# Lengths of keys and queries in the DeltaNet mixer: from a matrix of ones times the squares, in place of diagonal matrices of inverse lengths

## The reference, cut to what matters

```python
def _l2norm(x):
    xf = x.astype(jnp.float32)
    return (xf * lax.rsqrt(jnp.sum(xf * xf, axis=-1, keepdims=True) + EPS)).astype(x.dtype)

    b_qkv = jax.nn.silu(_dwconv_centred(b_qkv, conv_w))
    qb, kb, vb = jnp.split(b_qkv, 3, axis=-1)
    qb = _l2norm(qb.reshape(bsz, T, H_B, DK))
    kb = _l2norm(kb.reshape(bsz, T, H_B, DK))
```

## Time and profile before

| | |
|---|---|
| median of 3 runs | 1379.74 us (1378.78 to 1380.05) |
| the profiled execution | 1380.04 us |
| its span | 1378.3 us |
| PE busy | 1338.7 us (97%), 10242 instructions |
| DVE, ACT, POOL busy | 400.3, 282.4, 108.3 us |
| HBM | 499.86 MB, mean 363 GB/s |
| chain that ended last | PE 92%, DMA 4%, DVE 2%, ACT 1%, issue 1% |

### The profile page before, as it was taken

How to read it: one execution, slowest core, us unless ns; L and a number is a source line. 1 busy time by engine, 2 the same in 40 slices (tenths; PEclk the granted TensorE clock), 3 DMA queues, 4 the chain that set the end, 5 groups by cost and what they waited for, 6 DMA issues and landing times.

```text
span 1378.3 us, 23298 instructions
## 1 busy us (share of the span) xinstructions
PE 1338.7 (97%) x10242; PEld 705.6 (51%) x10242; DVE 400.3 (29%) x517; ACT 282.4 (20%) x364; POOL 108.3 (8%) x182
## 2 busy tenths in 40 slices
PE   4999999999999999999999999999999999999987
PEld 2997677678888885333333333333333333333332
DVE  2856344666444454101201400401101100100213
ACT  2673534453344333000000000000000000000011
POOL 6200141324000001000000000000000000010010
PEclk9999999999999999999999999999999999999998
DMA  9854967988777779999999999999999999999995
GB/s 382 306 161 152 379 252 277 405 311 301 244 244 245 260 293 416 363 360 427 427 423 430 427 422 412 424 410 430 424 426 429 425 425 427 428 423 427 425 428 239
DMA packets 103750, 499.86 MB, mean 363 GB/s; under 512 B 10514, under 2 KB 14303, under 8 KB 74855
## 3 DMA queue, kind: packets, MB, share of 16 engines
q1 hardware_dynamic: 87664, 471.75, 84.7%
q10 hardware_dynamic: 13590, 18.29, 3.7%
q0 software_dynamic: 2400, 8.42, 1.5%
HBM read 478.74 MB, written 19.69 MB: 362 GB/s over the span
## 4 chain that ended last, share of the span: by engine, by line
PE 92%; DMA 4%; DVE 2%; ACT 1%; issue 1%; ACTq 0%; DVEq 0%; SPq 0%
PE ps L2523 21%; PE ps L2520 17%; PE ps L2550 15%; PE ps L458 5%; PE ps L460 5%; PE ps L459 5%; PE ps L2557 4%; DMA ring_a<-in_moe_down 3%; PE ps L1927 3%; PE ps L1913 2%; PE ps L2059 1%; PE ps L2060 1%; PE ps L2061 1%; PE ps L2203 1%; PE ps L2016 1%; DMA raw<-in_w_mod 1%
## 5 line engine op out<-in xcount | busy, mean ns | idle before, releaser
L399 DVE TENSOR_TENSOR w_lo<-raw,w_hi 128x2048 fp32r<-128x2048 f32 x60 | 144.8, 2416 | 124.2 <-ACT w_hi L395 124.2
L2523 PE MATMUL ps<-ring_a,hTf 128*32 128x512 f32 (+1 forms) x1488 | 146.7, 551 | 0.0
L395 ACT ACTIVATE w_hi<-raw 128x2048 fp32r<-128x2048 f32 x59 | 112.8, 1914 | 108.7 <-PE ps L460 99.8
L2520 PE MATMUL ps<-raw,hTf 128*64 128x512 f32 (+1 forms) x624 | 123.8, 552 | 0.9 <-DMA raw<-in_moe_up 0.9
L1862 DVE TENSOR_TENSOR hm<-gate_bc,ps 32x384 f32<-32x384 f32 (+1 forms) x56 | 34.0, 607 | 267.5 <-PE ps L2520 266.6
L1868 DVE TENSOR_TENSOR hm<-gate_bc,ps 128x384 f32<-128x384 f32 (+1 forms) x16 | 9.4, 588 | 345.5 <-PE ps L2523 345.3
L2523 PEld LDWEIGHTS ps<-ring_a,hTf 128*32 128x32 f32 x1488 | 47.9, 110 | 96.9 <-issue 93.9
L458 PE MATMUL ps<-w_hi,hTh 128*128 128x512 f32 x232 | 91.5, 394 | 0.0
L460 PE MATMUL ps<-w_lo,hTh 128*128 128x512 f32 x232 | 90.4, 389 | 0.0
L459 PE MATMUL ps<-w_hi,hTl 128*128 128x512 f32 x232 | 90.3, 389 | 0.0
L2520 PEld LDWEIGHTS ps<-raw,hTf 128*64 128x64 f32 x624 | 44.1, 137 | 78.0 <-issue 74.9
(11 more groups left out here) (429 smaller groups left out, 1776.1 us busy)
## 6 DMA issues: line engine op xcount, KB each, us to landing
raw<-in_w_mod SPq DMA_DIRECT2D x48, 1024.0 KB, 7.8
raw<-in_moe_down SPq DMA_DIRECT2D x22, 2048.0 KB, 22.6
ring_a<-in_moe_down SPq DMA_DIRECT2D x20, 2048.0 KB, 19.1
ring_a<-in_moe_up SPq DMA_DIRECT2D x14, 2048.0 KB, 18.8
raw<-in_moe_gate SPq DMA_DIRECT2D x13, 2048.0 KB, 18.3
ring_b<-in_moe_down SPq DMA_DIRECT2D x13, 2048.0 KB, 19.5
ring_a<-in_moe_gate SPq DMA_DIRECT2D x11, 2048.0 KB, 24.6
raw<-in_moe_up SPq DMA_DIRECT2D x10, 2048.0 KB, 15.5
```

The lines of the kernel that those rows point to most:

```text
L395: nc.scalar.activation(w_hi[:, w % SPLIT], raw[:, slot % RAW], ACT.Copy).then_inc(s["hi_ready"], 1)
L399: nc.vector.tensor_tensor(w_lo[:, w % SPLIT], raw[:, slot % RAW], w_hi[:, w % SPLIT].bitcast(F32), ALU.subtract).then_inc(s["lo_ready"], 1)
L2520: last = MM(ps[HB * j:HB * j + HB, part % 4, 0:w], xT[:, kt, HB * (g // 2):HB * (g // 2) + HB], wt[:, kt % 2, 2 * (g % 2) + j, :], start=k ...
L2523: last = MM(ps[TOK * j:TOK * j + TOK, part % 4, 0:w], xT[:, KT * g + kt], wt[:, kt % 2, j, :], start=kt == 0, stop=kt == KT - 1)
```

## The change

The sums are spread at once: PE multiplies the matrix of ones, now the stationary side, with 512 columns of squares, which gives the sum over the channels in every partition. ACT takes square roots of 128x1024 from PSUM to `XT`, keys and queries apart, DVE takes reciprocals of 128x1024 in place, and multiplies. The diagonal matrices (DVE and POOL), `spread_lengths`, and the semaphores `len_diag`, `len_inverse`, `len_turned` go. On DVE the multiplications now stand ahead of `unit_lo` 14 and 15.

```diff
-            pool.wait_ge(s["len_inverse"], 1)
-            nc.gpsimd.tensor_tensor(XT[:, 0:8], rep(ident[:, :], 1, 8), rep(sm[:, 17, 0:8], 2, P), ALU.mult)\
-                .then_inc(s["len_diag"], 1)
...
             unit_hi(act, 13)
-            act.wait_ge(s["ss_turned"], 2)
-            nc.scalar.activation(sm[:, 16], ps[:, 6, 0:16], ACT.Sqrt, bias=eps[:, 0:1]).then_inc(s["rq_ready"], 1)
+            for first, bank in ((8, 2), (0, 6)):
+                act.wait_ge(s["ss_turned"], 1 if bank == 2 else 2)
+                nc.scalar.activation(flat2(XT[:, first:first + 8]), flat2(ps[:, bank:bank + 2]), ACT.Sqrt, bias=eps[:, 0:1])\
+                    .then_inc(s["rq_ready"], 1)
             copy_proj(5)
...
+            qv = b_ch[:, 0:4].rearrange("p a (c n) -> p (a c) n", n=P)
+            kv = b_ch[:, 4:8].rearrange("p a (c n) -> p (a c) n", n=P)
             dve.wait_ge(s["rq_ready"], 1)
-            nc.vector.reciprocal(sm[:, 17], sm[:, 16]).then_inc(s["len_inverse"], 1)
-            dve.wait_ge(s["len_inverse"], 1)
-            VT(XT[:, 8:16], rep(ident[:, :], 1, 8), rep(sm[:, 17, 8:16], 2, P), ALU.mult).then_inc(s["len_diag"], 1)
+            step(nc.vector.reciprocal(XT[:, 8:16], XT[:, 8:16]))
+            VT(kv, kv, XT[:, 8:16], ALU.mult).then_inc(s["kn_ready"], 1)
+            dve.wait_ge(s["rq_ready"], 2)
+            step(nc.vector.reciprocal(XT[:, 0:8], XT[:, 0:8]))
+            nc.vector.scalar_tensor_tensor(qv, qv, DK ** -0.5, XT[:, 0:8], ALU.mult, ALU.mult).then_inc(s["qn_ready"], 1)
             unit_lo(dve, WOUT)
             unit_lo(dve, WOUT + 1)
...
-            dve.wait_ge(s["len_turned"], 1)
-            VT(kv, kv, inv[:, 8:16], ALU.mult).then_inc(s["kn_ready"], 1)
-            dve.wait_ge(s["len_turned"], 2)
-            nc.vector.scalar_tensor_tensor(qv, qv, DK ** -0.5, inv[:, 24:32], ALU.mult, ALU.mult).then_inc(s["qn_ready"], 1)
...
-            def square_sums(first):
+            def square_sums(first, bank):
 
                 pe.wait_ge(s["sq_ready"], 1)
+                pe.wait_ge(s["cols_saved"], 4)
                 pe.wait_ge(s["diff_ready"], 2)
-                for i in range(first, first + 8):
-                    last = MM(ps[:, 6, i:i + 1], X[:, i], ones[:, 0:1], start=True, stop=True)
+                for h in range(2):
+                    last = MM(ps[:, bank + h, :], ones[:, :], flat(X[:, first + 4 * h:first + 4 * h + 4]), start=True, stop=True)
                 last.then_inc(s["ss_turned"], 1)
-
-            def spread_lengths():
-
-                pe.wait_ge(s["len_diag"], 2)
-                pe.wait_ge(s["cols_saved"], 4)
-                for i, bank in ((2, 2), (3, 3), (0, 6), (1, 7)):
-                    last = MM(ps[:, bank, :], ones[:, :], flat(XT[:, 4 * i:4 * i + 4]), start=True, stop=True)
-                    if i % 2:
-                        last.then_inc(s["len_turned"], 1)
...
                         if n == 10:
-                            square_sums(8)
-                        if n == 12:
-                            spread_lengths()
+                            square_sums(0, 6)
...
                 if i == 4:
-                    square_sums(0)
+                    square_sums(8, 2)
```

More of the change, by code:

```diff
@@ L157 @@
 hc_lo hi_ready hT_by_scalar hT_by_vector htok_turned k_saved k_turned kd_ready kdf_ready kn_ready ks_turned
-ktok_saved ktok_turned kv_y_stored L_beta L_masked L_turned late_saved late_sel late_turned len_diag
-len_inverse len_turned lo_ready logits_saved logits_turned LT_saved m1_saved m1_turned mask_ready
+ktok_saved ktok_turned kv_y_stored L_beta L_masked L_turned late_saved late_sel late_turned
+lo_ready logits_saved logits_turned LT_saved m1_saved m1_turned mask_ready
 mod_cols_saved mod_cols_turned mod_rows_copied mod_used mx_ready o_b_turned o_turned oa_ready p_exp p_in
@@ L1484, in _ @@
                 unit_lo(dve, i)
+            qv = b_ch[:, 0:4].rearrange("p a (c n) -> p (a c) n", n=P)
+            kv = b_ch[:, 4:8].rearrange("p a (c n) -> p (a c) n", n=P)
             dve.wait_ge(s["rq_ready"], 1)
-            nc.vector.reciprocal(sm[:, 17], sm[:, 16]).then_inc(s["len_inverse"], 1)
-            dve.wait_ge(s["len_inverse"], 1)
-            VT(XT[:, 8:16], rep(ident[:, :], 1, 8), rep(sm[:, 17, 8:16], 2, P), ALU.mult).then_inc(s["len_diag"], 1)
+            step(nc.vector.reciprocal(XT[:, 8:16], XT[:, 8:16]))
[3 more added lines that the diff above has]
+            nc.vector.scalar_tensor_tensor(qv, qv, DK ** -0.5, XT[:, 0:8], ALU.mult, ALU.mult).then_inc(s["qn_ready"], 1)
             unit_lo(dve, WOUT)
             unit_lo(dve, WOUT + 1)
-            qv = b_ch[:, 0:4].rearrange("p a (c n) -> p (a c) n", n=P)
-            kv = b_ch[:, 4:8].rearrange("p a (c n) -> p (a c) n", n=P)
-            inv = ps.rearrange("p a (c n) -> p (a c) n", n=P)
-            dve.wait_ge(s["len_turned"], 1)
-            VT(kv, kv, inv[:, 8:16], ALU.mult).then_inc(s["kn_ready"], 1)
-            dve.wait_ge(s["len_turned"], 2)
-            nc.vector.scalar_tensor_tensor(qv, qv, DK ** -0.5, inv[:, 24:32], ALU.mult, ALU.mult).then_inc(s["qn_ready"], 1)
             dve.wait_ge(s["decay_ready"], 2)
```

## The result

The changed kernel takes 1381.8 us (median of 20 runs, 1379.87 to 1383.44), the kernel before 1379.45 us (20 runs). The ratio is 1.0014, 95% interval 1.0008 to 1.0020: 1.1 to 2.8 us slower, small, but clear of no change. I had forecast 0.3 us less, and no measurable change. The profiled execution took 1381.64 us with a span of 1379.9.

What follows compares the result with a forecast made beforehand. PE alone was taken to bound 98 to 153 us. It saves 3.57 us and gives back 3.2 waiting for DVE, net 0.3: profiled 1380.04 to 1379.7, median 1379.4, stated as 1379.5; range 1378.3 to 1384.0 us.

Steps and rivals of the forecast that it cites:

- PE's own saving: On PE, `spread_lengths` goes and ones products replace the one-column sums: 3.57 us saved, all on the chain.
- ACT and POOL at nothing: ACT's larger square roots fit ahead of its copy at 113.0 and POOL's dropped 2.93 us were hidden: no cost, no gain.
- The reciprocals, D = 6.2 us: On DVE, each of two 128x1024 reciprocals takes 6.2 us, from slopes of narrow rows carried to 1024 columns.
- My own formula, 2 x (D - 6.36): Net time change in us from D, the time of one wide DVE reciprocal, down to a floor of -3.57.
- The place where PE would wait, and on what: PE waits 1.2 us for `qn_ready` ahead of `key_products(0)`, then 2.0 us for DVE's `L_masked` ahead of `key_products(1)`.
- The dearer reciprocal, 8.7 us: Rival: a wide DVE reciprocal makes eight passes a column, 8.7 us each, +4.7 us, time 1384.4; chance 0.16.
- Softmax just in time: DVE's later list still lets `turn_probs(1)` and `turn_probs(2)` start in time, within 0.3 us; costed at nothing to 0.3.
- Moved units hidden: `unit_lo` 14 and 15 move later on DVE, delaying two modulation loads 9 and 6.6 us; hidden with 5 us over.
- PE's clock: Rival: PE's new gaps lower its granted clock behind `L_masked`, losing 1.7 us, time 1381.1; chance 0.10.
- the prediction's signs of being wrong: Reciprocals' mean over 7.7 or under 4.8 us, `turn_probs(1)` starting later than before, or granted clock falling in 133 to 140.

Runs made afterwards that it cites:

- ln_exp: Changed kernel with DVE's reciprocals replaced by ScalarE computing exp(-0.5 ln(sum + eps)); ratio 0.9983 to the kernel before, span 1376.9 us.
- units_later: Changed kernel with `unit_lo` 14 and 15 moved behind `mask_keys(0)` on DVE; ratio 1.0004 to the kernel before, span 1379.6 us.
- fill_first: Changed kernel with two unused products added on PE only in its first gap, ahead of `key_products(0)`; ratio 1.0013 to the kernel before, span 1379.7 us.
- fill_second: Changed kernel with two unused products added on PE only in its second gap, ahead of `key_products(1)`; ratio 1.0021 to the kernel before, span 1381.3 us.
- extra_512: Changed kernel with one more reciprocal of 128x512, of values no longer read, on DVE ahead of `unit_lo` 14; ratio 1.0046 to the kernel before, span 1385.0 us.
- fill_both: Changed kernel with four unused products added on PE, two in each of its two gaps; ratio 1.0006 to the kernel before, span 1380.1 us.
- after_again: The changed kernel traced a second time with nothing altered, to see whether the clock's fall repeats; span 1378.0 us.
- widths: Changed kernel with reciprocals of eight widths (8 to 1024 columns) and some products added after all DVE work; time not compared, 1024 against 512 columns 3198 ns more.

## Why the prediction was wrong, step by step

- **PE's own saving, 3.57 us: right.** `ln_exp` shows it whole, 3.56 us at both `key_products`.
- **ACT and POOL at nothing: right.** The two roots ran from 108.87 to 110.99 and ScalarE still idled 1.80 us before its next copy.
- **The reciprocals, D = 6.2 us: the term that was mis-sized.** They took 6.55 each. My own formula, 2 x (D - 6.36), gives +0.4 for that, and the traces without a clock loss on the path show +0.4 to 0.5 at `hTh`. Both of my slopes, 6.1 and 5.7 ns, lay under 6.25: carried to 1024 columns they gave 6.4 and 6.0 us, the 6.2 between them lies under the 6.36 at which the sign turns, and the measured 6.55 lies over it. The rows could not decide the sign. From 4 columns (176 ns) to 16 the row of 252 ns gives 6.3 ns a column and 6.6 us, that of 246 ns gives 5.8 and 6.1 us: 6 ns between two rows of 16 columns become 0.5 us at 1024, and 1 us in the result. So the forecast of 0.3 us less was inside what the rows left open. The place where PE would wait, and on what, was right: the two gaps were forecast as 1.2 and 2.0 us and came as 1.98 and 1.74, the beta products and mask at 129.9 and 132.2 in place of 129.2 and 131.5.
- **The dearer reciprocal, 8.7 us: refuted.** The Trainium skill, VectorE: DVE Perf Modes, section "Walkthrough: the 8-slice pipeline in each mode", speaks of a repeat count of 8; read as eight passes it would be 8.35 ns a column, and 6.25 were measured. The measurement decides: six times an ordinary product's 1.04, not eight.
- **Softmax just in time: right.** `turn_probs(1)` and `(2)` had no wait on DVE in the changed kernel.
- **Moved units hidden: right** at their place, with little over, as `units_later` shows by moving them 3.5 us further.
- **PE's clock, left out of the sum, with a chance of 0.10 and 1.7 us: the size was right, the chance too small.** I had one row, a gap of 2.51 us, and took gaps of 1.2 and 2.0 as mostly safe. In the traces here, gaps of 1.7 to 2.0 us were followed by a fall in four of seven traces (the changed kernel two of three, `fill_first` one of one, `fill_second` one of two, `units_later` none of one); `extra_512`, with 5.4, fell as well. It costs time on the path only if PE's list is the last to arrive behind it. One of the prediction's signs of being wrong is this fall in 133 to 140; it came in the first trace. The other that came is `turn_probs(1)`, which starts at 143.72 there and at 142.29 and 142.23 in the other two traces, in place of 141.71.

The sum of both, 0.4 and a larger part of 1.7, would lie inside the measured 1.1 to 2.8 us. But only one of three traces paid the clock's 1.7 us on the path; as a mean that makes 0.4 + 0.6 = 1.0 us, an estimate from three traces, and just under the interval. How often the clock falls in the 20 runs is not known. Their mean granted clocks (0.995 to 0.998) take in falls in other places and don't go with the times: the eight runs at 0.995 have the median of all 20, 1381.8. The last loads shift single executions by more than a microsecond. So the failed steps are D, 6.2 in place of 6.55 us, which alone turns -0.3 into +0.4, and the clock, which the sum left out; how the rest of the measured 1.9 us, about 1.5, divides between the clock and the last loads stays open. That `fill_both`, without gaps, is only 0.06% over the kernel before, where the changed kernel is 0.14% over it, points to the clock, but their intervals overlap.

## What to carry to other kernels

A saving on the busiest engine is worth no more than the slack of the engine that feeds it next: add the new work to that engine's list instruction by instruction, and look which wait ends last. Replacing narrow values by values already spread over all partitions multiplies every elementwise step after it by the width; an operation that is cheap at 16 columns (0.25 us) may be six times an ordinary one per column at 1024 (6.55 us), so look for its rows at several widths. Rows at 4 and 16 columns don't fix a time at 1024 to better than half a microsecond; where the sign of the sum hangs on less than that, say that the sign is open. And a new gap on TensorE has a second price, its clock, which is paid in some executions and is to be kept in the range.

## What the runs showed of the hardware that I had not expected

- The granted clock fell behind single gaps of 1.74 us and 1.98 us, and with the same program and the same gaps in another execution it did not. Each fall cost 1.7 us of full-speed time (0.58 over 4 us in `fill_second`; 0.70, 0.50, 0.94 over 6 us in the changed kernel).
- A fall is free where the slow work runs into a wait that follows it (after_again).
- A reciprocal on VectorE costs 6.25 ns a column from 16 to 1024 columns (`widths`), six times an ordinary product's 1.04. In `ln_exp` two ln and two exp of 128x1024 on ScalarE take 2.27 and 2.01 us, with a table load of 1.28 us ahead of each pair.
